# The end of the attention: who combines the last two units, in which order ScalarE reads, and the scalar operand of GpSimd

## The reference, cut to what matters

```
for each block of 128 queries, for each of 4 heads:
    sc   = q[m] @ k[m]^T * scale          for the two maps m = 0, 1
    p[m] = softmax(causal(sc))            over up to 2048 keys
    a    = p[0] - lam * p[1]
    o    = a @ v
ya  = rms_norm(o) * (1 - lam_init)
mix = concat(ya, yb, yc, yd) @ w_out
x   = x + g1 * mix                        then norm, MLP, and a second residual
```

## Time and profile before

| | before |
|---|---|
| three runs | 2299.97 (median), 2299.58, 2304.3 us |
| the profiled execution | 2298.87 us, of which the trace's span is 2297.0 us |
| busy, share of the span | PE 2205.9 us (96%), PEld 1852.7 (81%), DVE 1845.1 (80%), ACT 1121.8 (49%), POOL 358.8 (16%) |
| mean granted PE clock | 0.99 |
| the attention | about 490 to 841 us of the span; the stretch of the change is 818 to 861 us |

### The profile page before, as it was taken

How to read it: one execution, slowest core, us unless ns; L and a number is a source line. 1 busy time by engine, 2 the same in 40 slices (tenths; PEclk the granted TensorE clock), 3 DMA queues, 4 the chain that set the end, 5 groups by cost and what they waited for, 6 DMA issues and landing times. The chain is left out here.

```text
span 2297.0 us, 29815 instructions
## 1 busy us (share of the span) xinstructions
PE 2205.9 (96%) x11258; PEld 1852.7 (81%) x11258; DVE 1845.1 (80%) x2593; ACT 1121.8 (49%) x1787; POOL 358.8 (16%) x285
## 2 busy tenths in 40 slices
PE   6999999987999999999999999998999999999998
PEld 4988897866889888878888788887888888878887
DVE  6548796989989886788887998877688777898887
ACT  4532554448888864433333545443353333545442
POOL 0343043843455640000000000000000000000000
PEclk9999999989999999999999999999999999999999
DMA  7441435130000035268888544447334444644444
GB/s 270 161 161 47 145 122 165 37 106 29 15 10 29 10 113 185 92 212 290 279 279 318 193 147 155 152 155 264 108 120 164 154 153 152 239 164 138 165 138 174
DMA packets 185738, 345.10 MB, mean 150 GB/s; under 512 B 11496, under 2 KB 83452, under 8 KB 184572
## 3 DMA queue, kind: packets, MB, share of 16 engines
q1 hardware_dynamic: 185508, 343.16, 43.9%
q10 hardware_dynamic: 88, 0.04, 0.0%
HBM read 236.20 MB, written 106.95 MB: 149 GB/s over the span
## 5 line engine op out<-in xcount | busy, mean ns | idle before, releaser
L2965 PE MATMUL ps<-sb_h_hi 128*128 128x512 f32 x512 | 200.2, 391 | 8.1 <-ACT ps L1712 3.8
L2967 PE MATMUL ps<-sb_h_hi,sb_h_lo 128*128 128x512 f32 x512 | 199.3, 389 | 0.0
L2966 PE MATMUL ps<-sb_h_lo,sb_h_hi 128*128 128x512 f32 x512 | 199.2, 389 | 0.0
L2931 PE MATMUL ps<-sb_h_hi,sb_w_hi 128*128 128x512 f32 x448 | 176.5, 394 | 5.0 <-DVE sb_u_full L2403 5.0
L2614 PE MATMUL ps<-sb_h_hi,sb_w_hi 128*128 128x512 f32 x448 | 177.5, 396 | 0.7 <-DVE sb_w_lo L2237 0.7
L2932 PE MATMUL ps<-sb_h_lo,sb_w_hi 128*128 128x512 f32 x448 | 175.3, 391 | 0.0
L2616 PE MATMUL ps<-sb_h_hi,sb_w_lo 128*128 128x512 f32 x448 | 174.5, 389 | 0.0
L2615 PE MATMUL ps<-sb_h_lo,sb_w_hi 128*128 128x512 f32 x448 | 174.4, 389 | 0.0
L2118 DVE TENSOR_SCALAR_CACHE_REDUCE sb_scores<-ps 128x1024 f32<-128x1024 f32 (+7 forms) x160 | 139.6, 891 | 12.3 <-PE ps L2828 6.7
L2965 PE MATMUL ps<-sb_w_hi 128*128 128x512 f32 x384 | 149.4, 389 | 0.0
L2966 PE MATMUL ps<-sb_w_lo,sb_w_hi 128*128 128x512 f32 x384 | 149.4, 389 | 0.0
(11 more groups left out here) (342 smaller groups left out, 5922.3 us busy)
## 6 DMA issues: line engine op xcount, KB each, us to landing
left_scratch<-sb_u_sum SPq DMA_DIRECT2D x128, 256.0 KB, 6.2
sb_right<-w_gated_scratch SPq DMA_DIRECT2D x16, 2048.0 KB, 8.8
sb_h_lo_full<-left_scratch SPq DMA_DIRECT2D x64, 512.0 KB, 3.8
sb_w_full<-in_w_ff SPq DMA_DIRECT2D x28, 1024.0 KB, 6.4
left_scratch<-sb_u_full SPq DMA_DIRECT2D x96, 256.0 KB, 2.5
sb_w_full<-left_scratch SPq DMA_DIRECT2D x48, 512.0 KB, 3.3
sb_w_raw<-in_w_in SPq DMA_DIRECT2D x16, 1024.0 KB, 5.8
sb_ada<-in_w_ada SPq DMA_DIRECT2D x32, 512.0 KB, 5.1
```

The source lines that it names most:

```text
L2931: M(psum[:, bank, :], wh[:, k, :], rh[:, k, :], start=fresh and k == 0, stop=False, skip_group_check=True)
L2965: M(dst, hi[:, k, tok], hi[:, 2 + k, :], start=fresh and k == 0, stop=False, skip_group_check=True)
L2966: M(dst, hi[:, k, tok], low[:, 2 + k, :], start=False, stop=False, skip_group_check=True)
L2967: ins = M(dst, low[:, k, tok], hi[:, 2 + k, :], start=False, stop=k == 1, skip_group_check=True)
```

## The change

Four edits. DVE combines units 62 and 63 (`LATE` = 62 and on) in two instructions, the second for the columns that GpSimd did; GpSimd leaves them out; PE waits for the second of two `a_ready` steps instead of `upper_ready`. ACT's list of the last two steps is written out by hand, with `w_out` parts 0 and 1 split in halves of 128x1024 (`wo_head_half`), one behind a read each. DVE does `wo_tail(0, 0)` ahead of `mix_tail(1)`. And GpSimd's multiplication, which is left for units 28 to 61, becomes a `tensor_scalar` with the ratio column as its scalar operand and a second multiplication by 1.0.

```
-UPPER_NO = running(int(upper(u) < len(at_groups(u))) for u in range(UNITS))
+LATE = UNITS - 2
+UPPER_NO = running(int(upper(u) < len(at_groups(u))) for u in range(LATE))
+def combined_no(u, part):
+    return u + 1 if u < LATE else 2 * u - LATE + part + 1
...
-                    link(pool.tensor_tensor(out=z, in0=z, in1=ratio[:, u % 4, 1:2].to_broadcast([P, n - c0]), op=ALU.mult))
+                    link(pool.tensor_scalar(z, z, ratio[:, u % 4, 1:2], 1.0, ALU.mult, ALU.mult))
...
-                if u >= 2 and u - 2 < UNITS:
+                if 0 <= u - 2 < LATE:
                     combine_upper(u - 2)
...
+            def wo_head_half(i, a, before):
+                act.wait_ge(*wo_loaded(0, i))
+                act.wait_ge(*before)
+                ins = A(by_k2(wo_hi(0, i))[:, a, :], by_k2(wo_raw(0, i))[:, a, :], ACT.Copy)
+                if a:
+                    ins.then_inc(whi_ready, 1)
...
+            items = at_items(UNITS + 1)
+            read_turn(items[0])
+            read_turn(items[1])
+            act.wait_ge(sc_mm, SC_NO[UNITS])
+            mix_head(0)
+            read_turn(items[2])
+            wo_head_half(0, 0, (at_mm, turned(UNITS - 3)))
...
-                if both and UPPER_NO[u] >= 4:
+                if u >= LATE:
+                    dve.wait_ge(upper_ready, UPPER_NO[LATE] - 3 + u - LATE)
+                elif both and UPPER_NO[u] >= 4:
                     dve.wait_ge(upper_ready, UPPER_NO[u] - 3)
...
+                if u >= LATE:
+                    rest = (u // HEADS + 1) * P - n
+                    V.scalar_tensor_tensor(out=prob(u, 0, n, rest), in0=prob(u, 1, n, rest), scalar=ratio[:, s, 1:2],
+                                           in1=prob(u, 0, n, rest), op0=ALU.mult, op1=ALU.add).then_inc(a_ready, 1)
...
             mix_tail(0)
+            wo_tail(0, 0)
             mix_tail(1)
-            wo_tail(0, 0)
             wo_tail(0, 1)
...
                     if f == 0:
-                        pe.wait_ge(a_ready, i + 1)
+                        pe.wait_ge(a_ready, combined_no(i, 0))
                     if f == upper(i):
-                        pe.wait_ge(upper_ready, UPPER_NO[i] + 1)
+                        if i < LATE:
+                            pe.wait_ge(upper_ready, UPPER_NO[i] + 1)
+                        else:
+                            pe.wait_ge(a_ready, combined_no(i, 1))
```

More of the change, by code:

```diff
@@ L1523, in _ @@
                     exp_of(u - 1, 0)
-                for n, x in enumerate(items[:early]):
+                if u > UNITS:
+                    continue
+                for x in items[:early]:
                     read_turn(x)
[L1526 to L1529, removed]
                 if 0 <= u - 1 < UNITS:
                     exp_of(u - 1, 1)
-                for n, x in enumerate(items[early:]):
-                    if n == 0 and u == UNITS + 1:
-                        wo_head(0, 0, (at_mm, turned(UNITS - 3)))
+                for x in items[early:]:
                     read_turn(x)
-                if u == UNITS + 2:
-                    wo_head(0, 1, (at_mm, turned(UNITS - 2)))
+            items = at_items(UNITS + 1)
[5 more added lines that the diff above has]
+            wo_head_half(0, 0, (at_mm, turned(UNITS - 3)))
+            read_turn(items[3])
+            wo_head_half(0, 1, (at_mm, turned(UNITS - 3)))
+            items = at_items(UNITS + 2)
+            read_turn(items[0])
+            mix_head(1)
+            read_turn(items[1])
+            wo_head_half(1, 0, (at_mm, turned(UNITS - 2)))
+            read_turn(items[2])
+            wo_head_half(1, 1, (at_mm, turned(UNITS - 2)))
+            read_turn(items[3])
             wo_head(0, 2, (at_mm, turned(UNITS - 1)))
```

## The result

The changed kernel takes 2288.42 us (median of four runs, 2285.33 to 2289.81) where the kernel before takes 2300.18 (four runs, 2299.58 to 2304.3): a ratio of 0.9942, 95% interval 0.9929 to 0.9954, some 11.8 us. The forecast was 2294.9 with a range down to 2292.0, so the direction is right and the size is not. The profiled execution of the changed kernel takes 2289.81 us, its span is 2287.8 and its mean granted clock 0.992.

The account below looks back on a forecast made before the run. PE, busy 96% of the span, was taken as the bound, so only its idle time could be won: 3.7 us at the attention's end plus 1.4 from GpSimd, 5.1 off the median 2299.97, gave 2294.9 us; range 2292 to 2298.3.

Parts of the forecast that it names:

- The head of part 1 is ready 3.7 us earlier, the DVE chain moves by as much: End of attention: ACT finishes part 1's head at 837.41 instead of 841.12, moving DVE's chain to 860.28 by 3.7 us.
- GpSimd 1.4: GpSimd's scalar-operand multiplication shortens PE's waits for its additions: 1.4 us, between 2.5 and a loss of 1.0.
- DVE's added work is hidden: Units 62 and 63: one more DVE instruction of 1.28 us each ends before PE or the first `mix_tail` needs it.
- The exchange costs nothing: Swapping `wo_tail(0, 0)` and `mix_tail(1)` on DVE is free, since PE reads tile 1 only after 849.
- A shift at 860 reaches the end: Behind 861 PE's idle time starts only from its own queue for a long stretch, so the gain reaches the end.
- So DVE decides at 860: At 860 us PE alone could come up to 4.3 us earlier, so DVE's chain sets the gain, 3.7 us.
- I take 0.9 of the 1.2 us off the wait: At 770 us, two GpSimd multiplications each 0.6 us shorter take 0.9 us off PE's wait of 2.49.
- The sum of 5.1: Whole kernel: 3.7 us from the attention's end plus 1.4 from GpSimd, taken off the median of 2299.97.
- Rival 3: GpSimd's hold-ups vanish in more units than counted, giving 3 us or more: 2291.5 to 2293; chance 0.11.
- Rival 1: Only the end pays; at 770 hold-ups just swap order, PE's part up to 0.7 us later: 2296.3 to 2297; chance 0.16.
- Rival 2: ACT's instructions don't overlap across kinds, costing 0.60 and 1.06 us, leaving 2.4 of the 3.7: 2296.2; chance 0.09.
- Rival 4: Slower: the scalar operand makes GpSimd's multiplication much longer, 4 ns a column giving 2310 us; chance 0.04.

Follow-up runs that it names:

- ts_only: The kernel before with only GpSimd's multiplication changed to the scalar-operand form; 0.9991 of the kernel before.
- end_only: The kernel after without the scalar operand: GpSimd multiplies by the broadcast ratio as before, the new attention end stays; 0.9969 of the kernel before.
- after_again: The kernel after, unchanged, run again for a second trace and more times; 2290.78 us, 0.9956 of the kernel before.
- act_alone: The kernel after, but GpSimd combines the upper part of units 62 and 63 again; 2288.78 us, 0.9957 of the kernel before.
- dve_alone: The kernel before with one edit alone, DVE combining units 62 and 63 whole; 1.0006 of the kernel before.
- before_early: The kernel before with PE turning the identity in its waits at 264 and 462 us alone; 1.0010 of the kernel before.
- before_832: The kernel before with PE turning the identity 16 times in its wait at unit 63, ACT's order unchanged; 0.9983 of the kernel before.
- before_third: The kernel before, unchanged, run for one more trace; one time, 2302.13 us.
- after_kept: The kernel after with PE turning the identity in four waits (264, 462, 1019, 1570 us); 2284.89 us, 0.9938 of the kernel before.
- before_all_kept: The kernel before with PE turning the identity in six waits (264, 462, 770, 1019, 1570 us, unit 63); 2294.05 us, 0.9980 of the kernel before.
- after_fold: The kernel after with DVE's addition that PE waits for moved ahead of the folded-weight multiplication (feed-forward, 1011 us); 2280.49 us, 0.9918 of the kernel before.

## Why the prediction missed

From all traces, each row from DVE's timeline and the windows (us; "fall": the clock falls behind the wait; kernels with a filling in a stretch left out there; `ts_only` has the wait of after at 770 and that of before at unit 63, `end_only` the other way round):

| | waits of before | waits of after |
|---|---|---|
| unit 0 to unit 63, no fall at 770 | 321.35, 321.47, 321.40, 321.63 | 319.46, 319.34, 318.25, 319.59, 319.85, 318.56, 319.86, 319.79, 318.35 |
| the same, with a fall at 770 | 323.59, 323.38, 323.67, 323.63 | none |
| mean | 322.51 | 319.23 |
| unit 63 to the first normalised tile, no fall at 832 | 33.21 | 29.52, 29.51, 29.52, 29.54, 29.53, 30.73, 30.97, 29.53, 30.79 |
| the same, with a fall at 832 | 36.02, 36.62, 36.13, 36.12, 36.67, 39.44 | none |
| mean | 36.32 | 29.96 |

(30.7 and more stand where ACT waits 1.1 to 1.3 us for the load of its first `mix_in` tile.) The means differ by 3.28 and 6.36, 9.6 us together, where the timed runs give 9.7 (`after_again`) and 11.8. Unit 0 starts at 503.8 in the mean of six traces of one side and at 502.6 of the other; from the tile to DVE's last instruction it is 1431.9 (seven) and 1431.4 (six). No more of the gain lies there than the scatter of the executions.

The first rows mix two things. Every trace has half clock at the start of the attention, until 10.7 to 11.6 us behind unit 0's reciprocal or until 8.3 to 8.9. All four traces with a fall at 770 are of the second kind, and so are the three of after with 318.25 to 318.56. Like against like, GpSimd's edit gives 1.8 us (321.46 and 319.65 in the mean) without a fall at 770 and 5.2 (323.57 and 318.39) with it: the fall costs some 3.4 us, not the 2.1 between the rows.

- *The head of part 1 is ready 3.7 us earlier, the DVE chain moves by as much*: right against the trace that it was read from, 3.69. *GpSimd 1.4*: 2.0 between the first two traces, within its bounds; 0.2 us + 0.9 ns a column nearly held (694 ns for 512, 1.13 us for 1024), and at 770 us 1.1 came off the wait where 0.9 was taken. *DVE's added work is hidden*: right by `act_alone` and `dve_alone`. *The exchange costs nothing*: not tried by itself, but DVE waits 0.87 us for part 1's head behind it. *A shift at 860 reaches the end*: right in the mean, though PE does wait 3.6 us for DVE at 1019.
- The step that failed is the size of the two terms, 3.7 and 1.4, and in both for one reason: the price of a wait of PE was read from one trace in which, by luck, the clock stayed at 1.00 behind it. "The head of part 1 thus is ready at 837.41 instead of 841.12" takes 841.12 for the kernel before. In six of seven traces with the wait at unit 63 the clock falls behind it, ACT's reads follow PE's groups at half clock, and part 1's tail starts 2.8 to 5.2 us later; in the mean the term is 6.4 us. "I take 0.9 of the 1.2 us off the wait" takes the wait at 770 as its length; with the fall that four of eight traces have behind it, the term is 3.3 in the mean. "So DVE decides at 860" was right: in every trace PE waits for DVE's tile, except `before_early`. It does not protect from PE's pace, since DVE's chain starts with ACT's head and that stands behind the groups.
- The sum of 5.1 was then taken off the median of the runs, of which, by their share in the traces, most will have such a fall. The trace of before had neither of the two, but it had others, behind waits of 2.67, 3.42, 3.60 and 4.91 us (264, 462, 1019, 1569); the prediction didn't read them.
- Shown by an experiment is the fall at unit 63 (`before_832`). The one at 770 is read from traces alone: no run fills that wait by itself. And the pair with the waits filled stays 9.2 us apart and not 5.7, so a part of the 9.7 to 11.8 us may have a cause that is not found here.
- The rivals: none is what happened. Rival 3 has the time nearest, and GpSimd's part does come to some 3 us in the mean of the traces, but not by hold-ups that vanish: in `ts_only` DVE's ratio instruction is held up (over 0.3 us) in 13 units as before, 11.3 us in all where it was 15.4, and the rest is the fall at 770. Rival 1 is out: the wait at 770 fell. Rival 2 is out: ACT's instructions overlap, a read takes 0.48 us. Rival 4 is out: 1024 columns take 1.13 us.
- Open stays when a wait has a fall behind it: the same wait of 2.66 to 2.68 us at 264 us has one in five of twelve traces. The Trainium skill, TensorE: Matmul & The Clock Gate, Part 1 (The HAM clock gate), says that what the gate goes by runs on freely and doesn't start anew with a kernel; that the same wait has a fall in one execution and none in another agrees, but no row shows the gate itself.

## What to carry to other kernels

Where PE bounds a kernel, read the granted clock behind every wait of PE that a change takes away, and take a second trace of the unchanged kernel where a few us matter: one trace without a fall proves nothing. A wait is worth its length and, in the share of executions that have a fall, what the work at half clock delays on the chain that ends last. Here taking one away gave 6.4 us in the mean where one trace showed 3.7. Look for that chain's start: DVE was the last at 860, and still PE's pace counted, through ACT. A fall can also cost nothing, as the one at 570 did. Whether a change that adds such a wait costs as much was not tried.

## What was not expected of the hardware

- In some executions the clock falls to 0.50 behind waits of 1.9 to 2.1 us (462 us, unit 63), for 3.4 to 17 us. A few falls stand behind shorter waits: 1.29 us at 523 (`before_third`), and waits of 0.8 us for DVE's scores at 567 to 570 in five of 18 traces, 6.8 us each.
- Turning the identity in the wait kept the clock at 1.00 at each of six places. Whether that lessens the scatter is not shown: `after_kept` has 1.9 us in five runs and `after_again` 5.4 in five, but `before_all_kept` 7.7 in eleven, and `after_fold`, with no filling, 1.5 in four.
- GpSimd's `tensor_scalar` with its scalar out of memory runs like the one with constants: 694 ns for 512 columns against 665.
